# Attention scores of the second mixer issued in pairs on the two row halves of TensorE

## The reference

```python
q = q.reshape(B, S, N_GROUPS, HEADS_PER_GROUP, HEAD_DIM)      # 3 groups, 8 heads, 64 wide; k and v the same
for g, (window, dilation) in enumerate(((128, 1), (512, 4), (2048, 16))):
    o_g, lse_g = dilated_window_attention(q[:, :, g], k[:, :, g], v[:, :, g], tab_g, window, dilation)
alpha = softmax(stack(lses), axis=0)                          # over the three groups
o = sum(alpha * outs)                                         # 8 heads of 64
y_attn = o @ w_attn_out
merged = sigmoid(g_conv) * y_conv + sigmoid(g_attn) * y_attn
x = x + gate * (merged @ w_o)
```

## Time and profile before

| | us |
|---|---|
| median of 3 runs (lowest to highest) | 2762.75 (2760.8 to 2763.23) |
| the profiled execution's own time | 2762.24 |
| its span in the trace | 2760.2 |
| TensorE busy | 2680.5 (97%) |
| VectorE busy | 1980.6 (72%) |
| ScalarE busy | 1298.3 (47%) |

### The profile page before, as it was taken

How to read it: one execution, slowest core, us unless ns; L and a number is a source line. 1 busy time by engine, 2 the same in 40 slices (tenths; PEclk the granted TensorE clock), 3 DMA queues, 4 the chain that set the end, 5 groups by cost and what they waited for, 6 DMA issues and landing times.

```text
span 2760.2 us, 34115 instructions
## 1 busy us (share of the span) xinstructions
PE 2680.5 (97%) x13951; PEld 2240.7 (81%) x13951; DVE 1980.6 (72%) x2227; ACT 1298.3 (47%) x1451; POOL 0.8 (0%) x6
## 2 busy tenths in 40 slices
PE   6999999999999999999999999899999999999998
PEld 3887777888887777888888899778888879987887
DVE  4767878777768878877777767567777776756754
ACT  2444565544434556544444434454454454445443
POOL 0000000000000000000000000000000000000000
PEclk9999999999999999999999999899999999999999
DMA  7886854677687764677776759347768767753652
GB/s 271 286 293 214 289 184 167 234 262 259 238 291 246 281 220 154 219 261 260 242 258 224 267 199 301 112 136 265 260 216 281 253 238 247 245 182 109 236 198 92
DMA packets 324579, 634.20 MB, mean 230 GB/s; under 512 B 12355, under 2 KB 92419, under 8 KB 324425
## 3 DMA queue, kind: packets, MB, share of 16 engines
q1 hardware_dynamic: 311616, 619.73, 65.3%
q10 hardware_dynamic: 12808, 12.30, 1.5%
HBM read 630.88 MB, written 8.97 MB: 232 GB/s over the span
## 4 chain that ended last, share of the span: by engine, by line
PE 86%; DVE 9%; ACT 3%; issue 2%; DMA 1%; ACTq 0%; DVEq 0%; SPq 0%
PE bank L1407 18%; PE bank L1409 18%; PE bank L1408 18%; PE acc L1407 8%; PE acc L1409 7%; PE acc L1408 7%; DVE w_both L954 3%; PE acc L1584 1%; PE bank L1516 1%; ACT w_both L540 1%; PE bank L1644 1%; DVE softmax L1155 1%; DVE temp L1154 1%; DVE w_extra L954 1%; PE acc L1627 1%
## 5 line engine op out<-in xcount | busy, mean ns | idle before, releaser
L954 DVE TENSOR_TENSOR w_both<-raw,w_both 128x2048 fp32r<-128x2048 f32 x412 | 941.6, 2290 | 506.6 <-ACT w_both L540 503.2
L540 ACT ACTIVATE w_both<-raw 128x2048 fp32r<-128x2048 f32 x412 | 786.6, 1913 | 651.1 <-PE bank L1409 363.7
L1407 PE MATMUL bank<-w_both,h 128*128 128x512 f32 (+1 forms) x2016 | 774.7, 384 | 4.0 <-DVE w_both L954 1.8
L1409 PE MATMUL bank<-w_both,h 128*128 128x512 f32 (+1 forms) x2016 | 760.3, 377 | 0.0
L1408 PE MATMUL bank<-w_both,h 128*128 128x512 f32 (+1 forms) x2016 | 759.6, 377 | 0.0
L1407 PEld LDWEIGHTS bank<-w_both,h 128*128 128x128 f32 x2016 | 381.1, 189 | 78.4 <-issue 6.5
L1409 PEld LDWEIGHTS bank<-w_both,h 128*128 128x128 f32 x2016 | 380.6, 189 | 71.2
L1408 PEld LDWEIGHTS bank<-w_both,h 128*128 128x128 f32 x2016 | 381.4, 189 | 67.3 <-issue 1.0
L988 DVE SCALAR_TENSOR_TENSOR ada_sum<-raw,c_act,ada_sum 128x512 f32<-128x512 f32 x476 | 357.5, 751 | 14.0
L1407 PE MATMUL acc<-w_both,y 128*128 128x512 f32 x896 | 355.4, 397 | 2.1 <-DVE temp L1194 1.4
L1409 PE MATMUL acc<-w_both,y 128*128 128x512 f32 x896 | 349.5, 390 | 0.0
(11 more groups left out here) (195 smaller groups left out, 2376.6 us busy)
## 6 DMA issues: line engine op xcount, KB each, us to landing
raw<-in_w_ada_all SPq DMA_DIRECT2D x136, 1024.0 KB, 5.2
raw<-in_w_in SPq DMA_DIRECT2D x128, 1024.0 KB, 5.5
raw<-in_ffn_gate_all SPq DMA_DIRECT2D x88, 1024.0 KB, 5.2
raw<-in_ffn_up_all SPq DMA_DIRECT2D x88, 1024.0 KB, 5.3
raw<-in_ffn_down_all SPq DMA_DIRECT2D x88, 1024.0 KB, 4.9
raw<-in_w_branch SPq DMA_DIRECT2D x12, 1024.0 KB, 6.8
raw<-in_w_out SPq DMA_DIRECT2D x8, 1024.0 KB, 5.0
raw<-in_w_conv_out SPq DMA_DIRECT2D x8, 1024.0 KB, 4.9
```

The costliest lines, as they stand in the source:

```text
L540: activate(halves_of[n][0], src, ACT.Copy).then_inc(high_ready.sem, 1)
L954: tensor(halves_of[n][1], raw_of("unit", s, k, 0)[0], halves_of[n][0].bitcast(F32), ALU.subtract).then_inc(low_ready.sem, 1)
L1407: mm(dst, a_h, b_h, start=start, stop=False, skip_group_check=True)
L1409: return mm(dst, a_l, b_h, start=False, stop=True, skip_group_check=True)
```

## The change

The columns of the third group's q and k in `w_in_2` are laid out with the heads of each pair swapped, on the host: head m's third group lies in the lower rows where its first group lies in the upper ones, and the other way about. `scores(m)` of kind "b" then issues, for each half, group 0 and group 2 of head m one after the other (on different halves of the rows), and for even m also group 1 of head m and group 1 of head m + 1. So an even head issues eight products, an odd head four; the sum for two heads stays twelve. The scores of a group have a PSUM bank of their own; those of an odd head's second group lie in `acc[:, 1408:1536]` and in `small[:, 0:256]`. `scores_done` counts four for each head, and VectorE waits for all four before it adds the first bias. For an odd head VectorE adds the bias in two instructions for each half: one for group 1, one for groups 0 and 2.

```diff
         def score_places(kind, m):
             if kind == "b":
-                return acc[:, 1024:1408], acc[:, 0:768]
+                groups = acc[:, 0:1536].rearrange("p (g n) -> p g n", g=GROUPS2)
+                return groups[:, :, 0:P], groups[:, :, P:3 * P]
...
+        odd_scores = acc[:, 1408:1536], small[:, 0:S]
...
-        scores_done = signal("scores_done", 0, 32, 16)
+        scores_done = signal("scores_done", 0, 32, 32)
+        odd_added = signal("odd_added", 0, 0, 8)
...
-                        dve.wait_ge(scores_done.sem, scores_done.at(s, 2 * m + half + 1 if kind == "b" else
+                        dve.wait_ge(scores_done.sem, scores_done.at(s, 4 * m + 4 if kind == "b" else
                                                                     2 * (m - m % 2) + 4))
...
-                            linked(tensor(grouped(logit), grouped(score), bias, ALU.add))
+                            if kind == "b" and m % 2:
+                                tensor(grouped(logit)[:, 1, :], odd_scores[half], bias[:, 1, :], ALU.add
+                                       ).then_inc(odd_added.sem, 1)
+                                linked(tensor(grouped(logit)[:, 0:3:2, :], score[:, 0:3:2, :],
+                                              bias[:, 0:3:2, :], ALU.add))
+                                dve.wait_ge(odd_added.sem, odd_added.at(s, m + half))
+                            else:
+                                linked(tensor(grouped(logit), score if kind == "b" else grouped(score), bias, ALU.add))
...
+                def group_score(m, half, g):
+
+                    first = HEAD * ((m + (g == 2)) % 2)
+                    w = P * (1 + half)
+                    dst = odd_scores[half] if g == 1 and m % 2 else score_places(kind, m)[half][:, g, :]
+                    return mm(dst, proj[first:first + HEAD, 4 * g + m // 2, P * half:P * half + P],
+                              proj[first:first + HEAD, 12 + 4 * g + m // 2, 0:w], start=True, stop=True,
+                              skip_group_check=True)
+
+                def group_scores(m):
+
+                    for half in range(2):
+                        last = [group_score(m, half, 0), group_score(m, half, 2)]
+                        if m % 2 == 0:
+                            last = [group_score(m, half, 1), group_score(m + 1, half, 1)]
+                        last[0].then_inc(scores_done.sem, 1)
+                        last[1].then_inc(scores_done.sem, 1)
...
-                        for half in range(2):
-                            score(m, half).then_inc(scores_done.sem, 1)
+                        group_scores(m)
                         return
...
+    for c0 in (2 * QKV2 // 3, QKV2 + 2 * QKV2 // 3):
+        heads = arrays["w_in_2"][:, :, c0:c0 + QKV2 // 3]
+        heads[:] = heads.reshape(*heads.shape[:2], 4, 2, HEAD)[:, :, :, ::-1].reshape(heads.shape)
```

More of the change, by code:

```diff
@@ L1581, in score @@
                     w = P * (1 + half)
[L1582 to L1587, removed]
+                    qt, kt = (8, 12) if forget else (0, 4)
+                    return mm(dst[:, 0:w], proj[rows_, qt + h_no // 2, P * half:P * half + P],
+                              proj[rows_, kt + h_no // 2, 0:w], start=True, stop=not forget, skip_group_check=True)
+                def group_score(m, half, g):
[12 more added lines that the diff above has]
+                        last[1].then_inc(scores_done.sem, 1)
                 def forget_score(m, half):
@@ L1949 @@
         "ffn_down_all": np.concatenate([a["ffn_w_down"], a["ffn_w_down_2"]]),
-        "w_in": a["w_in"], "w_in_2": a["w_in_2"], "w_branch": a["w_branch"], "w_out": a["w_out"],
+        "w_in": a["w_in"], "w_in_2": a["w_in_2"].copy(), "w_branch": a["w_branch"], "w_out": a["w_out"],
         "w_pool": a["w_pool"], "forget_bias": a["forget_bias"].T.copy(),
```

## The result

The changed kernel takes 2745.44 us (median of 4 runs, 2744.3 to 2746.63) against 2761.85 for the kernel before (4 runs, 2760.8 to 2763.23): a ratio of 0.994 with a 95% interval of 0.9923 to 0.9958. Five later runs gave 2745.54 beside 2761.35 (15 runs), ratio 0.9943 (0.993 to 0.9957). So some 16 us are gained, clear of the 0.2% that count as no change; the forecast was 10.65 and the range ended at 2746.0, 0.6 us short. The profiled execution took 2744.3, its span is 2742.5, 17.7 less than before.

What follows compares the result with a forecast made beforehand. TensorE, busy 97% of the span, was taken to bound the kernel. One stage: 0.65 + 1.2 + 0.65 + 3 x 1.16 = 6.0 us; two 12.0, less one clock fall 10.65: 2752.1 of 2762.75, range 2746 to 2757.5.

Steps and rivals of the forecast that it cites:

- What bounds the kernel, and which heads count: Attention of stages 7 and 10: TensorE sets the pace except at heads 4 and 6, where VectorE does; those save nothing.
- What the pairs save: Scores on TensorE: odd heads take 0.86 us instead of 2.16, saving 1.30; even heads 1.51, saving 0.65.
- Rival (C): Pairs do not run side by side, leaving only six dearer adds, 0.8 us: 2763.6; chance 0.06.
- What the split adds cost: VectorE's bias adds, four instead of two for an odd head: 0.14 us more a head, at most 0.71.
- the straight line: Estimate of the 128x512 bias add, between the rows' 0.414 and 0.948 us: 0.68.
- Head 1: Clock stays at 0.50 until 9.0 us after the scores' start, as now: 1.2 us gained a stage, bounds nothing to 2.8.
- The falls: Clock drops to 0.50 at heads 4 and 6: one more counted, 1.35 us lost; bounds -2.7 to +2.7.
- Rival (D): Clock falls and stays at 0.50 some 10 us at heads 4 and 6 of both stages: 4.5 slower, 2767.2; chance 0.04.
- Head 5: Like heads 3 and 7: 1.30 us off TensorE less 0.14 for the adds, so 1.16 kept.
- rival (A): Clock comes back sooner at head 1 in both stages and no fall is added: 15.2 us gained, 2747.5; chance 0.16.

Runs made afterwards that it cites:

- same_rows: Changed kernel with the old rows: all three groups of a head on the same row half, one add per half; 2761.99 us, ratio to before 1.0002.
- pair_02: Against same_rows, only the rows differ: groups 0 and 2 of a head on different row halves, group 1 alone; 2751.43 us, ratio to before 0.9962.
- gate_early: Changed kernel with ScalarE's copy of the gate's second half moved to the start of its turn in the second mixer's attention; 2745.19 us.
- rows_apart: Changed kernel with an even head's products of a half ordered lower, lower, upper, upper; 2746.92 us.

## Why the prediction was right or wrong

**What bounds the kernel, and which heads count.** Right. 0-1 and 2-3 saved 0.64 to 0.67 each, 3-4 and 7-rows 1.18 to 1.19 (1.16 forecast), 4-5 and 6-7 nothing at full clock, with the idle time of 0.50 grown to 1.15. Six of the eight distances were right within 0.05 us in each stage, clock apart.

**What the pairs save.** Right: 0.86 and 1.51 us, taken from the pairs of the first mixer, and products of the two row halves start 0.01 us apart. "Up to 2x" of the Trainium skill's "TensorEngine Tiling (Array Packing)", Overview, would have had 1.08 for the mean head; the trace has 1.19, so the row was the better guide. The Trainium skill's "TensorE: Matmul & The Clock Gate", The cost: per-tile semaphore tail, has 26 ns for each further increment; no row shows a cost beyond the 0.86 that already holds them, and same_rows, which doubles them too, takes the time of before (1.0002). Rival (C) is excluded by these rows, and that the rows' halves are the cause is shown by pair_02 against same_rows.

**What the split adds cost.** Right. VectorE's timeline of the changed kernel, head 5 of stage 10:

```profile
2485.54 0.29 DVE L1160 TENSOR_TENSOR temp<-acc,bias_t 128x128 f32<-128x128 f32 x1 [0.56 <-PE acc L1653]
2485.74 0.41 DVE L1162 TENSOR_TENSOR temp<-acc,bias_t 128x256 f32<-128x256 f32 x1
2486.19 0.55 DVE L1167 TENSOR_REDUCE softmax<-temp 128x1 f32<-128x384 f32 x1
2486.66 0.41 DVE L1160 TENSOR_TENSOR temp<-bank,bias_t 128x256 f32<-128x256 f32 x1
2486.99 0.68 DVE L1162 TENSOR_TENSOR temp<-acc,bias_t 128x512 f32<-128x512 f32 x1
2487.71 0.95 DVE L1167 TENSOR_REDUCE softmax<-temp 128x1 f32<-128x768 f32 x1
2488.58 2.28 DVE L959 TENSOR_TENSOR w_both<-raw,w_both 128x2048 fp32r<-128x2048 f32 x1
```

From the first add to `low` it is 3.04 us, 2.91 before (2486.07 to 2488.98, head 3's; head 5's is 2.92): 0.13 a head, 0.14 forecast, and the 0.68 of the straight line is there. The first add of a half lies partly beside the second (0.20 from start to start at 0.29 long).

**Head 1: wrong, mis-sized.** "I take this stretch as it is", 9.0 us from the start of the scores, gave 1.2 us a stage; 2.43 and 2.76 were measured, 2.8 us more in all. The upper bound given there, "if it comes back 3 us sooner", is what came: a stretch is 3.4 us shorter. Over all profiles the clock came back 8.4 us after the start of the scores before and 5.3 after the change, in the mean, without overlap (7.0 to 9.4 against 3.8 to 6.4); the moment adds or takes 3.4 us of stretch besides. The row itself had the clock come back inside the gate unit, and that unit begins 2.5 us sooner now. Holding a clock event still while the work around it shrinks by 2.5 us was the mistake. What in that work brings the clock back these runs do not show.

**The falls: wrong in sign.** "I count one fall more", because TensorE would do less between two waits; none came and the two of the profile of before were gone: +1.35 forecast, -2.6 measured, 4.0 us. They aren't the kernel's rule: its second profile has none. They should have been entered as a part of the profile's own luck, to come off its time, with no forecast of more. That the two went is luck at least in part. Rival (D), with long falls at four places, is excluded: 0 in 9 profiles.

**Head 5: a wait not seen.** The sum gave it 1.16, it kept 0.87 and 0.89, 0.6 us in all the other way. Nothing in the sum asked what ScalarE had in its queue when the transposes came 1.30 us sooner; gate_early shows it.

So 10.65 + 2.8 + 4.0 - 0.6 = 16.9, the attention's saving. That is rival (A) (15.2) with the two falls of now gone (2.6), which it kept, and with 0.4 less at head 1 and 0.6 less at head 5; its chance of 0.16 was too low. The medians' 16.4 and 15.8 are less than the profiles' 17.7: the kernel before was profiled with two falls that its second profile lacks, and the changed one in the fastest of its four executions. What the clock did in the runs without a profile isn't known.

## What to carry to other kernels

Products of 64 rows on alternate halves of the rows took 0.86 and 1.51 us; all on one half they would take an estimated 1.51 and 2.8, with the 0.163 a pass of the rows. Here they also wrote different banks, and no run has them in one. Where another stage already runs such pairs, its start-to-start time gives the new one to 0.01 us. When an engine gets through sooner, go through the other engines' queues at that very place, here ScalarE's three instructions. And treat a clock stretch in one profile as one draw: take a second profile, or shift the work by some tenths of a microsecond, before a term of the sum leans on it. Write down beside it where in the work the clock fell and came back; if the change moves that work, move the clock's return with it.

## What the runs showed of the hardware that was not expected

The stretches at 0.50 in these attentions were 3.4, 6.8 or 10.2 us long, in 17 profiles. The same instructions at head 1 had two lengths 3.4 us apart, the longer one whenever the clock fell before the scores began, the shorter one when it fell up to 1.2 us after (32 of 32 stretches, both kernels); four executions had two lengths in their two stages. Products on the other half of the rows start beside those ahead of them even when another product stands between in the program (rows_apart: 1.61 us for eight, 1.51 when alternating).
